# Row spreads, sample-state outer products and sample-state products of a hybrid decoder step: fp32r and column tiles

## The chip, the cores and the metric

One core of one Trainium2 chip runs the whole program. The metric is the device time of one execution in microseconds. The kernel before took 1665.42 us (median of three runs, 1665.4 to 1666.57).

## What is computed

The reference is one decoder layer for 256 prompt tokens and 8 sample tokens (d_model 1024, 8 heads): a gated-delta branch (GDN) and a latent-attention branch (MLA) on one normalised input, merged by gates, then an MLP. All data is fp32. The change touches the recurrence of the samples, the row scalings of the GDN branch and one row scaling of the MLA branch:

```python
def gdn_recurrent(q, k, v, g, beta, s0):      # the samples: 8 tokens, 8 heads, one step
    s = jnp.exp(g_t)[..., None, None] * s
    u = b_t[..., None] * (v_t - jnp.einsum('bhk,bhkv->bhv', k_t, s))
    s = s + jnp.einsum('bhk,bhv->bhkv', k_t, u)
    return s, jnp.einsum('bhk,bhkv->bhv', q_t, s)

def l2_normalize(x):                          # q and k of GDN, per token and head
    return x * lax.rsqrt(jnp.sum(jnp.square(x), axis=-1, keepdims=True) + EPS)
```

Activations lie channel by token (128 partitions of channels, 264 columns of tokens: 256 prompt, 8 sample). A factor per token is therefore a row, and a row has to be spread over 128 partitions before VectorE can multiply by it.

## The kernel before

**Stages.** A front stage (to about 140 us) computes the down projections. Then 128 cache pages are worked off (to about 1314 us), and the last stage runs the gate, output and MLP matrices. TensorE's operands of the large products are split into a high and a low fp32r part, and three fp32r products stand for one of fp32.

**The page loop.** Each page n has two halves, and `keys(n, half)` issues 12 fp32r products of 512 columns for each (lines 1729 to 1731). In front of each half, `beside(i)` with i = 2n + half issues a piece of other work, on TensorE, VectorE and ScalarE alike. Every engine runs its own instruction list in order, and semaphores tie them. `beside` holds first the prompt attention (`front_pe`, i under 29), then from i = 35 four head pairs b = 0 to 3 of 52 slots k each (`pair_pe`, `pair_dve`, `pair_act`).

**Two side banks.** Products of `beside` go in turn to two PSUM banks in the order of the list SIDE_A. `begin_a(name)` waits until the bank's last user but one was read, `a_bank(name)` on VectorE waits for the product. Small transposes go through one more bank (SIDE_B).

**The places that the change touches**, by slot k of a pair:
- `spread_row` (line 1791): one fp32 product whose stationary operand is one column of the identity, broadcast to 128 columns; out comes a row on all partitions. Slots 18, 19 (`gr`, 64 rows of `rw`), 21, 22 (`br`, 64 rows), 23, 24 (`lb`, two each, 4 rows of `lr`), 51 (`ob`, two, 2 rows of `lr`): 10 in a pair. The same form stands at line 1941 for `nope` (16 rows of `nrow`, 256 columns, two in each of the slots i = 10 to 17).
- `newton` (lines 1209 to 1218): VectorE turns the square root of a row into its reciprocal with one Newton step; the `lb` spreads wait for the one of slot 22, the `ob` spreads for the one of slot 50.
- `kqs` (line 1890, slot 28): for each of 8 samples and 2 heads, the 128 x 128 sample state is the stationary operand and the two columns q and k are the moving one: 16 fp32 products of two columns.
- `krow`, `urow` (slots 30, 32): transposes of 16 columns; ScalarE copies the rows to `urow`.
- `state_out` (line 1808, slots 40, 42, 45, 47): k outer u for four state blocks at once, one fp32 product with 16 rows of contraction and 512 columns. `masked_rows` (line 1324) zeroes the rows of u that belong to other blocks.

An fp32 product stands in the trace as two records (it streams its columns twice), an fp32r product as one.

Of the kernel before, what the change touches and what calls it, by code (L numbers as in the profile page):

```python
# [21 lines left out]
P = 128  # L22
D = 1024
TP = 256
# [45 lines left out]
C_LVT = _col(P)  # L70
C_ALL = _at


def constants():

    c = np.zeros((P, C_ALL), np.float32)
    k, m = np.arange(P)[:, None], np.arange(P)[None, :]
    c[:, C_ID] = k == m
    c[:, C_BD] = k // 64 == m // 64
    c[:, C_ROT] = np.where((k == m + 32) & (m % 64 < 32), -1.0, 0) + ((k == m - 32) & (m % 64 >= 32))  # L80
    c[:, C_ONE] = 1.0
    inv = np.power(np.float32(10000.0), -np.arange(0, ROPE, 2, dtype=np.float32) / np.float32(ROPE)).astype(np.float32)
    pos = np.concatenate([np.arange(TP), np.full(NS, PAST)]).astype(np.float32)
# [12 lines left out]
    c[0:8, C_RSC] = SCALE  # L96
    c[8:16, C_RSC] = 1
    c[0:2, C_RSQ] = 128 ** -0.5
    c[2:4, C_RSQ] = 1
    c[:, C_LVT] = c[:, C_LVL[0]].T  # L100
    return c
# [14 lines left out]
PAIR_A = ([f"p{j}" for j in range(6)] + ["gr0", "gr1", "l2r", "br0", "br1", "lb0", "lb1", "lb2", "lb3", "qk", "kk", "qks", "x0", "x1", "kqs", "t1", "u1"])  # L116
# [39 lines left out]
def build(nc, I, O):  # L156
    C_in, ctx = I["consts"], ExitStack()
    with ctx:
# [35 lines left out]
        qeff, e = place("qeff", [P, NS, 5, 16], F32, taken["rsq"][0])  # L194
        assert e <= taken["rsq"][1]
# [49 lines left out]
        ltok = [place("ltok0", [P, LW], F32, taken["ukT01"][0])[0], place("ltok1", [P, LW], F32, taken["ukT67"][0])[0], place("ltok2", [P, LW], F32, taken["sq"][0])[0]]  # L245
        nrow, e2 = place("nrow", [16, T], F32, taken["sq"][0] + 4 * T * 4)
# [16 lines left out]
        assert e <= C_NEG.stop * 4  # L263
        lr, e = place("lr", [8, 2, T], F32, taken["krT"][0])
# [30 lines left out]
        bwl, o = place("bwl", [P, KC, P], F32R, o)  # L295
        rw, o = place("rw", [64, T], F32, o)
# [11 lines left out]
        sm, o = place("sm", [P, 8, 2 * NS], F32, o)  # L308
        lt3, o = place("lt3", [8, T], F32, o)
# [16 lines left out]
        umask, e = place("umask", [16, 4, P], F32, e)  # L326
        urow, e = place("urow", [16, 2, P], F32, e)
# [276 lines left out]
        def _(act):  # L604
# [159 lines left out]
            def pair_act(b, k):  # L764
# [37 lines left out]
                if k == 30:  # L802
                    nc.scalar.activation(urow[:, 0, :], rows_out(f"krow_{b}")[0:16, 0:P], ACT.Copy).then_inc(S("b_read"), 1)
                if k == 32:
                    nc.scalar.activation(urow[:, 1, :], rows_out(f"urow_{b}")[0:16, 0:P], ACT.Copy).then_inc(S("b_read"), 1)
# [110 lines left out]
        def _(v):  # L916
# [180 lines left out]
            def front_dve(i):  # L1097
# [42 lines left out]
                if i == 9:  # L1140
                    V.tensor_copy(snew[:], a_bank("snew")[:, 0:64]).then_inc(S("a_read"), 1)
# [20 lines left out]
            def decay_steps(i):  # L1162
# [17 lines left out]
                if i == 4:  # L1180
                    pair_low(0)
                if i == 5:
                    V.tensor_copy(bg[:].rearrange("p n c -> p (n c)"), a_bank("bg")[:, 0:128]).then_inc(S("a_read"), 1)

# [49 lines left out]
            def pair_dve(b, k):  # L1234
# [46 lines left out]
                if k == 25:  # L1281
                    V.tensor_tensor(dt_[:], four(bank("qk")), dt_[:], ALU.mult).then_inc(S("a_read"), 1)
                    V.tensor_tensor(lT[:], four(bank("kk")), lT[:], ALU.mult).then_inc(S("a_read"), 1)
                    v.wait_ge(S("a_read"), a_count(f"lb3_{b}"))
                    V.tensor_copy(small(1), sample_of(2)).then_inc(S("sample_ready"), 1)
                    V.tensor_tensor(small(2), sample_of(0), sample_of(2), ALU.mult).then_inc(S("sample_ready"), 1)
                if k == 26:
# [7 lines left out]
                    link(V.scalar_tensor_tensor(col2[:, 0:2], colb[:, 0, 1, :], -1.0, bg[:, 1, 2 * b:2 * b + 2], ALU.mult, ALU.mult))  # L1295
                if k == 27:
# [6 lines left out]
                if 28 <= k < 40 and k % 2 == 1:  # L1303
# [3 lines left out]
                    V.tensor_tensor(U_[:], U_[:], four(bank(f"u{s_}")), ALU.subtract).then_inc(S("a_read"), 1)  # L1307
                if k == 28:
                    kq = bank("kqs")[:, 0:4 * NS].rearrange("p (s h t) -> p s h t", s=NS, t=2)
                    egs = eg[:, :, TP:T].rearrange("p h s -> p s h")  # L1310
                    V.tensor_tensor(small(3), kq[:, :, :, 1], egs, ALU.mult)
                    V.tensor_tensor(small(4), kq[:, :, :, 0], egs, ALU.mult).then_inc(S("a_read"), 1)
                    v.wait_ge(S("a_read"), a_count(f"kqs_{b}"))
                    link(V.tensor_tensor(small(3), sample_of(4), small(3), ALU.subtract))
                    V.tensor_tensor(small(5), small(3), small(7), ALU.mult).then_inc(S("sample_ready"), 1)
# [5 lines left out]
                def masked_rows(m):  # L1321
                    v.wait_ge(S("b_read"), b_count(f"urow_{b}"))
                    v.wait_ge(S("conv_out"), 32 * b + 32)
                    V.tensor_tensor(umask[:], urow[:, 1, :].unsqueeze(1).to_broadcast([16, 4, P]),
                                    consts[0:16, C_ID.start + 4 * m:C_ID.start + 4 * m + 4].unsqueeze(2).to_broadcast([16, 4, P]), ALU.mult).then_inc(S("umask_ready"), 1)
# [267 lines left out]
        def _(pe):  # L1593
# [196 lines left out]
            def spread_row(name, rows_, col, moving):  # L1790
                a_done(mm(begin_a(name)[:, 0:T], consts[0:rows_, C_ID.start + col:C_ID.start + col + 1].to_broadcast([rows_, P]), moving, start=True, stop=True))  # L1791

            def pair_pe(b, k):
# [38 lines left out]
                if k in (18, 19):  # L1832
                    pe.wait_ge(S("g_ready"), 1)
                    pe.wait_ge(S("beta_ready"), 1)
                    spread_row(f"gr{k - 18}_{b}", 64, 32 + 2 * b + k - 18, rw[:])
# [6 lines left out]
                if k in (21, 22):  # L1842
                    spread_row(f"br{k - 21}_{b}", 64, 2 * b + k - 21, rw[:])
# [6 lines left out]
                if k in (23, 24):  # L1850
                    pe.wait_ge(S("row_rstd"), 2 * b + 1)
                    for c in range(2 * (k - 23), 2 * (k - 23) + 2):
                        spread_row(f"lb{c}_{b}", 4, c, lr[0:4, 0])
# [4 lines left out]
                if k == 26:  # L1858
# [24 lines left out]
                if k == 28:  # L1883
                    pe.wait_ge(S("sst_landed"), 16 * NS * (b + 1))
                    qks = qkv[:, 0:4, :].rearrange("p (t h) n -> p h n t", t=2)
                    p_ = begin_a(f"kqs_{b}")
                    for s_ in range(NS):
                        for hh in range(2):
                            at_ = 2 * (2 * s_ + hh)
                            i = mm(p_[:, at_:at_ + 2], sst[:, s_, hh, :], qks[:, hh, TP + s_, :], start=True, stop=True)  # L1890
                    a_done(i)
                if k == 30:
                    b_done(nc.tensor.transpose(begin_b(f"krow_{b}")[0:16, 0:P], sm[:, 1], ident))
                if k == 32:
                    pe.wait_ge(S("sample_ready"), 4 * b + 3)
                    b_done(nc.tensor.transpose(begin_b(f"urow_{b}")[0:16, 0:P], sm[:, 5], ident))
# [37 lines left out]
                if k == 51:  # L1934
                    pe.wait_ge(S("row_rstd"), 2 * b + 2)
                    for hh in range(2):
                        spread_row(f"ob{hh}_{b}", 2, hh, lr[0:2, 0])

            def front_pe(i):
# [47 lines left out]
                if F_NOPE <= i < F_NOPE + H:  # L1987
                    for n_ in (0, H):
                        h = n_ + i - F_NOPE
                        a_done(spread(begin_a(f"nope{h}")[:, 0:TP], nrow[:, 0:TP], 16, h))  # L1990
# [214 lines left out]
```

## Time and profile before

| | |
|---|---|
| time, median of three | 1665.42 us |
| time of the profiled execution | 1668.4 us |
| its span, first to last instruction | 1666.6 us |
| PE busy | 1628.4 us |
| DVE, ACT, POOL busy | 886.2, 649.5, 201.6 us |
| mean granted TensorE clock | 0.990 |

The profiled execution is 1.8 us longer than its span and 3.0 us longer than the median. PE is TensorE's matmuls, DVE VectorE, ACT ScalarE, POOL GpSimd. Durations of matmul records overlap, since they include filling and draining; what a matmul costs is read from one start to the next start.

### The profile page before, as it was taken

To read this page: it belongs to the slowest core of one execution; us is meant where nothing else is said; L and a number is where in the kernel's file an instruction comes from. 1 tells how busy PE (TensorE), PEld (TensorE's weight loads), DVE (VectorE), ACT (ScalarE), POOL (GpSimd) and SP (SyncE) were. 2 spreads that over 40 slices of the span, in tenths; PEclk is the share of its full clock that TensorE was granted. 3 is DMA by queue.
4 is the path that set the end of the run, shared out by engine and by line. 5 is a ranking of instruction groups with operands and counts; after the bars stand their busy time and mean duration, and the time that the engine had idled before them with its cause. 6 is when DMAs were issued, how large, how long until landed. Compare 5 with 4: busy or idle time off the path is not lost.

```text
span 1666.6 us, 26110 instructions
## 1 busy us (share of the span) xinstructions
PE 1628.4 (98%) x10140; PEld 1331.9 (80%) x10140; DVE 886.2 (53%) x1636; ACT 649.5 (39%) x981; POOL 201.6 (12%) x104
## 2 busy tenths in 40 slices
PE   6899999999999999999999999999999999999998
PEld 5777777886877777877877877877877899999998
DVE  5855444455445555354555445545444565777643
ACT  2233356345324445223454234353334344344431
POOL 0000202111111211111111112111112200000000
PEclk9999999999999999999999999999999999999999
DMA  7421102421012321102320013211013346545551
GB/s 248 138 75 34 31 20 56 126 68 29 29 29 59 107 81 30 29 29 59 92 68 29 29 30 96 83 30 29 29 32 105 127 166 214 177 155 187 185 181 52
DMA packets 111621, 140.79 MB, mean 84 GB/s; under 512 B 13648, under 2 KB 60272, under 8 KB 111368
## 3 DMA queue, kind: packets, MB, share of 16 engines
q1 hardware_dynamic: 106902, 137.13, 26.3%
q10 hardware_dynamic: 4602, 2.05, 0.5%
q8 instruction: 79, 1.29, 0.3%
q14 instruction: 38, 0.31, 0.1%
HBM read 132.61 MB, written 6.74 MB: 84 GB/s over the span
## 4 chain that ended last, share of the span: by engine, by line
PE 93%; DVE 4%; ACT 1%; ACTq 1%; issue 0%; DVEq 0%
PE ps L1729 15%; PE ps L1731 14%; PE ps L1730 14%; PE ps L2125 5%; PE ps L2126 5%; PE ps L2127 5%; PE ps L1720 4%; PE ps L1765 2%; PE ps L1749 2%; PE ps L2071 1%; PE ps L1816 1%; PE ps L2072 1%; PE ps L1815 1%; PE ps L2073 1%; PE ps L1817 1%; PE ps L1791 1%
## 5 line engine op out<-in xcount | busy, mean ns | idle before, releaser
L1729 PE MATMUL ps<-ukh,cTh 128*128 128x512 f32 x1024 | 426.8, 417 | 0.1
L1048 DVE TENSOR_REDUCE kss<-ksq 128x4 f32<-128x512 f32 x256 | 175.5, 685 | 463.3 <-ACT ksq L690 462.9
L1731 PE MATMUL ps<-ukh,cTl 128*128 128x512 f32 x1024 | 404.7, 395 | 0.0
L1730 PE MATMUL ps<-ukl,cTh 128*128 128x512 f32 x1024 | 403.7, 394 | 0.0
L690 ACT ACTIVATE ksq<-ps 128x512 f32<-128x512 f32 x256 | 152.8, 597 | 564.9 <-PE ps L1731 564.8
L595 POOL TENSOR_TENSOR rk<-kss,mhalf 128x32 f32<-128x32 f32 x32 | 178.3, 5570 | 548.0 <-DVE kss L1423 548.0
L1729 PEld LDWEIGHTS ps<-ukh,cTh 128*128 128x128 f32 x1024 | 194.6, 190 | 61.4 <-issue 27.2
L1731 PEld LDWEIGHTS ps<-ukh,cTl 128*128 128x128 f32 x1024 | 194.3, 190 | 45.0
L1730 PEld LDWEIGHTS ps<-ukl,cTh 128*128 128x128 f32 x1024 | 195.3, 191 | 33.5
L1426 DVE TENSOR_TENSOR wl<-wraw,wh 128x2048 fp32r<-128x2048 f32 x44 | 100.8, 2291 | 76.3 <-ACT wh L877 76.1
L877 ACT ACTIVATE wh<-wraw 128x2048 fp32r<-128x2048 f32 x44 | 84.3, 1916 | 133.8 <-PE ps L2127 126.0
L1044 DVE TENSOR_TENSOR cTl<-cTr,cTh 128x512 fp32r<-128x512 f32 x128 | 87.9, 687 | 14.4 <-ACT cTh L684 13.8
L2125 PE MATMUL ps<-Ah,wh 128*128 128x264 f32 x320 | 91.1, 285 | 1.2 <-DVE wl L1426 1.2
L1720 PEld LDWEIGHTS ps<-consts_sb,craw 128*128 128x128 f32 x512 | 59.1, 141 | 41.4 <-issue 33.1
L2127 PE MATMUL ps<-Ah,wl 128*128 128x264 f32 x320 | 90.8, 284 | 0.0
L2126 PE MATMUL ps<-Al,wh 128*128 128x264 f32 x320 | 90.7, 283 | 0.0
L684 ACT ACTIVATE cTh<-cTr 128x512 fp32r<-128x512 f32 x128 | 80.8, 631 | 4.1
L1720 PE MATMUL ps<-consts_sb,craw 128*128 128x128 f32 x512 | 80.4, 279 | 0.8 <-ACT cTr L681 0.8
L681 ACT ACTIVATE cTr<-ps 128x512 f32<-128x512 f32 x128 | 76.1, 595 | 0.5 <-PE ps L1720 0.3
L2127 PE MATMUL ps<-Hh,wl 128*128 128x264 f32 x256 | 72.9, 285 | 0.0
L2125 PE MATMUL ps<-Hh,wh 128*128 128x264 f32 x256 | 72.8, 284 | 0.0
L2126 PE MATMUL ps<-Hl,wh 128*128 128x264 f32 x256 | 72.8, 284 | 0.0
(445 smaller groups left out, 2865.1 us busy)
## 6 DMA issues: line engine op xcount, KB each, us to landing
craw<-cache_mla SPq DMA_DIRECT2D x128, 288.0 KB, 3.1
wraw<-w_in SPq DMA_DIRECT2D x16, 1024.0 KB, 4.9
wraw<-w_up SPq DMA_DIRECT2D x16, 1024.0 KB, 5.4
wraw<-w_down SPq DMA_DIRECT2D x16, 1024.0 KB, 4.9
braw<-w_in SPq DMA_DIRECT2D x24, 512.0 KB, 3.8
sst<-state_gdn SPq DMA_DIRECT2D x32, 128.0 KB, 3.6
gdn_sample<-sst SPq DMA_DIRECT2D x32, 128.0 KB, 2.1
wraw<-w_ya SPq DMA_DIRECT2D x4, 1024.0 KB, 5.0
```

Source lines behind the costliest of these rows:

```text
L595: nc.gpsimd.tensor_tensor(rk[:, y], kss[:, y], mhalf[:], ALU.pow).then_inc(S("rk_ready"), 1)
L690: nc.scalar.activation(ksq[:, half_], ps[:, k % 3, :], ACT.Square).then_inc(S("ksq_ready"), 1)
L1044: V.tensor_tensor(cTl[:, n % 2], cTr[:, :, tokens(n)], cTh[:, n % 2].bitcast(F32), ALU.subtract).then_inc(S("ct_lo"), 1)
L1048: V.tensor_reduce(kss[:, n // 4 % 2, n % 4, 4 * half_:4 * half_ + 4], ksq[:, half_].rearrange("p (h d) -> p h d", h=4), AX, ALU.add).then_ ...
L1426: V.tensor_tensor(wl2[:, ns % 2], wraw2[:, (ns - NM) % 4], wh2[:, ns % 2].bitcast(F32), ALU.subtract).then_inc(S("w_lo"), 1)
L1720: k = nc.tensor.transpose(trp[:, c, :], craw[:, n % RING, P * c:P * c + P], ident)
L1729: mm(out, cTh[:, n % 2, c], ukh[:, c, cols], start=c == 0, stop=False)
L1730: mm(out, cTh[:, n % 2, c], ukl[:, c, cols], start=False, stop=False)
L1731: i = mm(out, cTl[:, n % 2, c], ukh[:, c, cols], start=False, stop=c == 3)
L2125: mm(out, w_hi, mh[:, kc, :], start=first and kc == 0, stop=False)
L2126: mm(out, w_hi, ml[:, kc, :], start=False, stop=False)
L2127: k = mm(out, w_lo, mh[:, kc, :], start=False, stop=last and kc == 3)
```

## The change

Five edits, in one diff:
1. `spread_row` issues two fp32r products into one accumulation, a high and a low part of the row; its stationary column comes from `idr`, a rounded copy of the identity. VectorE makes the parts with `split` (a copy and a subtraction): for `rw` once, for `nrow` once (slot i = 9), and for `lr` at the end of each `newton`, whose consumers now wait for the split. `nope` uses `spread_row` too.
2. `kqs` moves from slot 28 to slot 26. The q and k columns of the samples are gathered in `sm` (32 columns) and are the stationary operand, 8 columns at a time; the state is the moving operand, 4 fp32 products of 512 columns, each to its own 32 partitions of the bank.
3. VectorE copies that bank to `X_` (slot 26), TensorE transposes it (4 blocks, `kqsT`, slot 27), and VectorE picks the wanted entries (slot 27, as before in slot 28).
4. `krow` and `urow` transpose three copies of the 16 columns (96 columns, from `ksrc`, `usrc`). ScalarE writes them rounded to fp32r (`kst`, `ust`) and one third raw (`kraw`), and VectorE turns one third into the low part (slots 31, 33).
5. `state_out` becomes one fp32r product with 96 rows: k high with u high, k low with u high, k high with u low, stacked. `umask` is 96 rows of fp32r.

```diff
             def newton(rows_, count, scale, sem):
...
-                V.scalar_tensor_tensor(x, y, scale, t_, ALU.mult, ALU.mult).then_inc(S(sem), 1)
+                link(V.scalar_tensor_tensor(x, y, scale, t_, ALU.mult, ALU.mult))
+                split(x, lrh[0:rows_], lrl[0:rows_], sem)
...
                 if k == 26:
+                    V.tensor_copy(X_[:].rearrange("p u n -> p (u n)"), bank("kqs")).then_inc(S("a_read"), 1)
+                if k == 31:
+                    v.wait_ge(S("b_read"), b_count(f"krow_{b}"))
+                    V.tensor_tensor(kst[32:64], kraw[32:64], kst[32:64].bitcast(F32), ALU.subtract).then_inc(S("kst_ready"), 1)
...
-            def spread_row(name, rows_, col, moving):
-                a_done(mm(begin_a(name)[:, 0:T], consts[0:rows_, C_ID.start + col:C_ID.start + col + 1].to_broadcast([rows_, P]), moving, start=True, stop=True))
+            def spread_row(name, rows_, col, high, low, width=T):
+                out, one = begin_a(name)[:, 0:width], idr[0:rows_, col:col + 1].to_broadcast([rows_, P])
+                mm(out, one, high, start=True, stop=False)
+                a_done(mm(out, one, low, start=False, stop=True))
...
                 def state_out(m):
+                    pe.wait_ge(S("kst_ready"), b + 1)
                     pe.wait_ge(S("umask_ready"), 4 * b + m + 1)
-                    a_done(mm(begin_a(f"out{m}_{b}"), urow[:, 0, :], umask[:].rearrange("p h n -> p (h n)"), start=True, stop=True))
+                    a_done(mm(begin_a(f"out{m}_{b}"), kst[:], umask[:].rearrange("p h n -> p (h n)"), start=True, stop=True))
...
                     a_done(mm(begin_a(f"qks_{b}")[:, 0:2 * NS], ones, sm[:, 2], start=True, stop=True))
+                    pe.wait_ge(S("sst_landed"), 16 * NS * (b + 1))
+                    p_ = begin_a(f"kqs_{b}")
+                    for j in range(4):
+                        i = mm(p_[32 * j:32 * j + 8, :], sm[:, 0:2].rearrange("p a n -> p (a n)")[:, 8 * j:8 * j + 8],
+                               sst[:, 2 * j:2 * j + 2].rearrange("p s h v -> p (s h v)"), start=True, stop=True)
+                    a_done(i)
                 if k == 27:
                     read("kk")
                     four("x0", 4, lambda out, w: nc.tensor.transpose(out, lT[:, w, :], ident))
+                    read("kqs")
+                    four("kqsT", 4, lambda out, w: nc.tensor.transpose(out, X_[:, w, :], ident))
...
-                if k == 28:
-                    pe.wait_ge(S("sst_landed"), 16 * NS * (b + 1))
-                    qks = qkv[:, 0:4, :].rearrange("p (t h) n -> p h n t", t=2)
-                    p_ = begin_a(f"kqs_{b}")
-                    for s_ in range(NS):
-                        for hh in range(2):
-                            at_ = 2 * (2 * s_ + hh)
-                            i = mm(p_[:, at_:at_ + 2], sst[:, s_, hh, :], qks[:, hh, TP + s_, :], start=True, stop=True)
-                    a_done(i)
                 if k == 30:
-                    b_done(nc.tensor.transpose(begin_b(f"krow_{b}")[0:16, 0:P], sm[:, 1], ident))
+                    b_done(nc.tensor.transpose(begin_b(f"krow_{b}")[0:96, 0:P], ksrc[:].rearrange("p r c -> p (r c)"), ident))
```

## Rows read from the trace of the kernel before

**Rows 1.** The page's busy times: us, share of the span, instructions.

```profile
PE 1628.4 (98%) x10140; PEld 1331.9 (80%) x10140; DVE 886.2 (53%) x1636; ACT 649.5 (39%) x981; POOL 201.6 (12%) x104
```

**Rows 2.** Groups of instructions: form, xrecords | busy us, mean ns | idle.

```profile
L1808 PE MATMUL ps<-umask,urow 16*128 16x512 f32 x32 | 17.9, 640 | 0.0
L1941 PE MATMUL ps<-nrow,consts_sb 16*128 16x256 f32 x32 | 9.0, 400 | 0.0
```

**Rows 3.** Chain that ended last, pair 0 slot 24: start us, us, line, xrecords.

```profile
402.89 0.23 PE ps L1731
403.12 1.08 PE ps L1791 x4
404.20 0.43 PE ps L1729
```

**Rows 4.** The same chain, pair 0 slot 19: a single spread.

```profile
379.67 0.64 PE ps L1791 x2
380.31 0.43 PE ps L1729
```

**Rows 5.** The same chain, pair 0 slot 40: an outer product.

```profile
485.33 1.05 PE ps L1808 x2
486.38 0.43 PE ps L1729
```

**Rows 6.** The same chain: one fp32r product of 264 columns.

```profile
784.28 0.12 PE ps L1816
```

**Rows 7.** The same chain, pair 2 slot 28: the sample-state products.

```profile
912.96 3.47 PE ps L1890 x32
916.43 0.34 PE ps L1729
```

**Rows 8.** The same chain, pair 3: 512 fp32r columns at the lower clock.

```profile
1159.72 0.43 PE ps L1729
```

**Rows 9.** Stretches: us, busy us of PE, PEld, DVE, ACT, POOL; clock, DMA.

```profile
425.35:432.18 6.83, 6.83 (x21) 4.78 (x25) 0.61 (x4) 0.52 (x1) 0.00 (x0) 0.50 0.00 0
...
780.33:783.75 3.42, 3.42 (x9) 2.63 (x8) 0.42 (x1) 0.00 (x0) 0.00 (x0) 0.50 0.07 24
...
1159.21:1162.63 3.42, 3.42 (x11) 2.64 (x10) 0.00 (x0) 0.31 (x1) 0.45 (x1) 0.50 0.00 0
...
1265.00:1268.40 3.40, 2.65 (x11) 1.97 (x12) 2.80 (x6) 0.79 (x2) 0.00 (x0) 1.00 0.85 251
```

**Rows 10.** The chain again: a run of transposes, then products on four column tiles.

```profile
383.30 0.44 PE ps L1757 x4
...
388.55 1.00 PE ps L1765 x8
389.55 0.48 PE ps L1720 x3
```

**Rows 11.** Timeline, VectorE, end of the Newton step in pair 1 slot 50.

```profile
777.67 0.28 DVE L1217 TENSOR_SCALAR lt<-lt 2x264 f32<-2x264 f32 x1
778.00 0.42 DVE L1218 SCALAR_TENSOR_TENSOR lr<-lr,lt 2x264 f32<-2x264 f32 x1
```

**Rows 12.** Waits of TensorE: us in total, times, longest.

```profile
PE ps L1791 <- DVE lr L1218: 3.3, 4, 1.3
```

**Rows 13.** Timeline, both engines, pair 0 slots 50 and 51.

```profile
532.80 0.42 DVE L1218 SCALAR_TENSOR_TENSOR lr<-lr,lt 2x264 f32<-2x264 f32 x1
...
533.38 0.48 PE L1791 MATMUL ps<-lr,consts_sb 2*128 2x264 f32 x1
```

**Rows 14.** Timeline, both engines, pair 1 slots 22 and 23.

```profile
641.03 0.48 DVE L1218 SCALAR_TENSOR_TENSOR lr<-lr,consts_sb,lt 4x264 f32<-4x264 f32 x1
...
642.57 0.48 PE L1791 MATMUL ps<-lr,consts_sb 4*128 4x264 f32 x1
```

**Rows 15.** Timeline, both engines, pair 1 slots 26 and 27.

```profile
660.61 0.15 DVE L1295 SCALAR_TENSOR_TENSOR col<-colb,bg 128x2 f32<-128x2 f32 x1
...
661.44 0.38 PE L1867 MATMUL ps<-consts_sb,lT 128*128 128x128 f32 x2
```

More of the change, by code:

```diff
@@ L70 @@
 C_LVT = _col(P)
+C_THIRDS = _col(16)
 C_ALL = _at
@@ L100, in constants @@
     c[:, C_LVT] = c[:, C_LVL[0]].T
+    c[0:96, C_THIRDS] = k[0:96] % 32 == m[:, 0:16]
     return c
@@ L115 @@
 B_START, B_SLOTS = F_END + 6, 52
-PAIR_A = ([f"p{j}" for j in range(6)] + ["gr0", "gr1", "l2r", "br0", "br1", "lb0", "lb1", "lb2", "lb3", "qk", "kk", "qks", "x0", "x1", "kqs", "t1", "u1"])
+PAIR_A = ([f"p{j}" for j in range(6)] + ["gr0", "gr1", "l2r", "br0", "br1", "lb0", "lb1", "lb2", "lb3", "qk", "kk", "qks", "kqs", "x0", "kqsT", "x1", "t1", "u1"])
 for _s in range(2, LEVELS):
@@ L194, in build @@
         qeff, e = place("qeff", [P, NS, 5, 16], F32, taken["rsq"][0])
+        idr, e = place("idr", [64, 64], F32R, e)
         assert e <= taken["rsq"][1]
@@ L245, in build @@
         ltok = [place("ltok0", [P, LW], F32, taken["ukT01"][0])[0], place("ltok1", [P, LW], F32, taken["ukT67"][0])[0], place("ltok2", [P, LW], F32, taken["sq"][0])[0]]
+        nrowh, e2 = place("nrowh", [16, TP], F32R, taken["ltok0"][1])
+        assert e2 <= taken["ukT01"][1]
+        nrowl, e2 = place("nrowl", [16, TP], F32R, taken["ltok1"][1])
+        assert e2 <= taken["ukT67"][1]
         nrow, e2 = place("nrow", [16, T], F32, taken["sq"][0] + 4 * T * 4)
@@ L263, in build @@
         assert e <= C_NEG.stop * 4
+        rwh, e = place("rwh", [64, T], F32R, C_NEG.start * 4)
+        assert e <= C_NEG.stop * 4
+        lrl, e = place("lrl", [8, T], F32R, taken["krT"][0] + 4 * T)
         lr, e = place("lr", [8, 2, T], F32, taken["krT"][0])
@@ L295, in build @@
         bwl, o = place("bwl", [P, KC, P], F32R, o)
+        rwl, _ = place("rwl", [64, T], F32R, o)
         rw, o = place("rw", [64, T], F32, o)
@@ L308, in build @@
         sm, o = place("sm", [P, 8, 2 * NS], F32, o)
+        lrh, _ = place("lrh", [8, T], F32R, o)
         lt3, o = place("lt3", [8, T], F32, o)
@@ L325, in build @@
         uu, e = place("uu", [P, 2, CH], F32, e)
-        umask, e = place("umask", [16, 4, P], F32, e)
-        urow, e = place("urow", [16, 2, P], F32, e)
+        umask, e = place("umask", [96, 4, P], F32R, e)
+        kst, e = place("kst", [96, P], F32R, e)
+        ust, e = place("ust", [96, P], F32R, e)
+        kraw, e = place("kraw", [96, P], F32, max(e, taken["tail"][1]))
+        ksrc, e = place("ksrc", [P, 3, 32], F32, e)
+        usrc, e = place("usrc", [P, 3, 32], F32, e)
         assert e <= TOP, e
@@ L1140, in front_dve @@
                 if i == 9:
+                    V.tensor_copy(idr[:], consts[0:64, C_ID.start:C_ID.start + 64])
+                    split(nrow[:, 0:TP], nrowh[:], nrowl[:], "nope_split")
                     V.tensor_copy(snew[:], a_bank("snew")[:, 0:64]).then_inc(S("a_read"), 1)
@@ L1181, in decay_steps @@
                     pair_low(0)
+                    V.memset(ksrc[:], 0.0)
+                    V.memset(usrc[:], 0.0).then_inc(S("src_clear"), 1)
                 if i == 5:
                     V.tensor_copy(bg[:].rearrange("p n c -> p (n c)"), a_bank("bg")[:, 0:128]).then_inc(S("a_read"), 1)
+                    v.wait_ge(S("beta_ready"), 1)
+                    split(rw[:], rwh[:], rwl[:], "rw_split")
             def conv(b, j):
@@ L1284, in pair_dve @@
                     v.wait_ge(S("a_read"), a_count(f"lb3_{b}"))
-                    V.tensor_copy(small(1), sample_of(2)).then_inc(S("sample_ready"), 1)
+                    for j in range(2):
+                        V.tensor_copy(sm[:, 0:2].rearrange("p a (s h t) -> p (a s) h t", h=2, t=2)[:, :, :, j], sample_of(2 * j))
+                    if b == 0:
+                        v.wait_ge(S("src_clear"), 1)
+                    V.tensor_copy(ksrc[:, :, 0:16].rearrange("p r (s h) -> p r s h", h=2), sample_of(2).unsqueeze(1).to_broadcast([P, 3, NS, 2])).then_inc(S("sample_ready"), 1)
                     V.tensor_tensor(small(2), sample_of(0), sample_of(2), ALU.mult).then_inc(S("sample_ready"), 1)
@@ L1307, in pair_dve @@
                     V.tensor_tensor(U_[:], U_[:], four(bank(f"u{s_}")), ALU.subtract).then_inc(S("a_read"), 1)
-                if k == 28:
[L1309 to L1313, printed above, removed]
+                if k == 27:
+                    bank("kqsT")
+                    at_ = B_PAIR + SIDE_A.index(f"kqsT_{b}") % 2
+                    kq = ps[:, at_:at_ + 2, :].rearrange("p b n -> p (b n)")[:, 0:520].rearrange("p (i x) -> p i x", x=130)[:, :, 0:128]
+                    kq = kq.rearrange("p (a h) (j r) -> p a h j r", h=2, r=32)
+                    egs = eg[:, :, TP:T].rearrange("p h (j a) -> p a h j", a=2)
+                    V.tensor_tensor(sm[:, 3].rearrange("p (j a h) -> p a h j", a=2, h=2), kq[:, :, :, :, 1], egs, ALU.mult)
+                    V.tensor_tensor(sm[:, 4].rearrange("p (j a h) -> p a h j", a=2, h=2), kq[:, :, :, :, 0], egs, ALU.mult).then_inc(S("a_read"), 1)
+                if k == 28:
+                    v.wait_ge(S("a_read"), a_count(f"kqsT_{b}"))
                     link(V.tensor_tensor(small(3), sample_of(4), small(3), ALU.subtract))
-                    V.tensor_tensor(small(5), small(3), small(7), ALU.mult).then_inc(S("sample_ready"), 1)
+                    link(V.tensor_tensor(small(5), small(3), small(7), ALU.mult))
+                    V.tensor_copy(usrc[:, :, 0:16], sm[:, 5].unsqueeze(1).to_broadcast([P, 3, 2 * NS])).then_inc(S("sample_ready"), 1)
                 if k == 30:
@@ L1321, in masked_rows @@
                 def masked_rows(m):
-                    v.wait_ge(S("b_read"), b_count(f"urow_{b}"))
+                    v.wait_ge(S("ust_ready"), b + 1)
                     v.wait_ge(S("conv_out"), 32 * b + 32)
-                    V.tensor_tensor(umask[:], urow[:, 1, :].unsqueeze(1).to_broadcast([16, 4, P]),
-                                    consts[0:16, C_ID.start + 4 * m:C_ID.start + 4 * m + 4].unsqueeze(2).to_broadcast([16, 4, P]), ALU.mult).then_inc(S("umask_ready"), 1)
+                    V.tensor_tensor(umask[:], ust[:].bitcast(F32).unsqueeze(1).to_broadcast([96, 4, P]),
+                                    consts[0:96, C_THIRDS.start + 4 * m:C_THIRDS.start + 4 * m + 4].unsqueeze(2).to_broadcast([96, 4, P]), ALU.mult).then_inc(S("umask_ready"), 1)
                 def state_out(m):
@@ L1832, in pair_pe @@
                 if k in (18, 19):
[L1833 to L1835 removed]
+                    pe.wait_ge(S("rw_split"), 1)
+                    spread_row(f"gr{k - 18}_{b}", 64, 32 + 2 * b + k - 18, rwh[:], rwl[:])
                 if k == 20:
@@ L1987, in front_pe @@
                 if F_NOPE <= i < F_NOPE + H:
+                    pe.wait_ge(S("nope_split"), 1)
                     for n_ in (0, H):
                         h = n_ + i - F_NOPE
-                        a_done(spread(begin_a(f"nope{h}")[:, 0:TP], nrow[:, 0:TP], 16, h))
+                        spread_row(f"nope{h}", 16, h, nrowh[:], nrowl[:], TP)
                 if F_NOPE <= i < F_NOPE + 6:
```

20 lines of the change are left out of this document (14 added, 6 removed).

## The prediction, made before the changed kernel ran

> **What bounds the kernel now.** First the page's busy times [rows 1]: TensorE is busy in 98% of the span, VectorE in 53%, ScalarE in 39%. So a change pays what it takes off TensorE's own line, and it costs whatever makes TensorE wait. Next the groups of instructions [rows 2] for what the touched products are: all fp32, two records for each product. Their busy and mean times overlap with neighbours, so they are no price. The price is read from the chain that ended last, which in the page loop is TensorE almost without a break: each piece there is the time that it adds. Then the waits of TensorE [rows 12]: in the page loop it waits for only one thing, the Newton step that the `lb` and `ob` spreads need, 3.3 us in four waits. Last the stretches with their granted clock [rows 9]: 0.50, the lower level of 1.2 GHz, in stretches that begin right behind the sample-state products of `kqs`, and in one behind an `ob` spread.
>
> **What a block costs.** A product of the keys with 512 columns takes 0.23 us in the chain, one directly behind a spread or an outer product 0.43 [rows 3, 5]. So a block costs its own piece and 0.20. Two spreads: 1.08 + 0.20 = 1.28 for four records [rows 3]. One spread: 0.64 + 0.20 = 0.84 for two [rows 4]. The difference, 0.44 for two records, makes 0.22 a record, and 0.84 - 0.44 = 0.40 stays for each block whatever it streams: its edges. An outer product costs 1.05 + 0.20 = 1.25 [rows 5]. Its two records of 512 columns are 2 x 0.22 x 512/264 = 0.85, which again leaves 0.40.
>
> **Edit 1, the spreads.** An fp32r product of 264 columns costs 0.12 [rows 6]. A spread goes from two records of 0.22 to two of 0.12: it saves 0.20, and the edges stay, since the rows of contraction stay 64, 16, 4 and 2. The 40 spreads of the pairs (10 in each of four) save 8.0. The 16 of `nope` [rows 2] have 256 columns and save 0.19 each, 3.0. Sum 11.0 us. The row for 0.12 has 128 rows of contraction; none of the trace has fp32r with fewer. I take 0.12, and the other end is under the rivals.
>
> **Edit 5, the outer products.** 16 of them (32 records, [rows 2]) go from 1.25 to one fp32r product of 512 columns, 0.23 [rows 3]. Whether the edges of 0.40 stay with 96 rows no row shows: blocks of 2 to 64 rows have them, the keys with 128 rows don't. Without edges the saving is 1.02 each, 16.3 in all; with them 0.62 each, 9.9. I take 16.3, because 96 rows can't share the array with a second product, while up to 64 could, and keep 9.9 for the range. On this the Trainium skill has a rule (TensorEngine Tiling (Array Packing), Key Properties and Available Configurations): a change of tiling mode drains the engine, and there is row tiling for 64 and for 32 rows only. By it the edges go with 96 rows, which is the 16.3; by the nearest row alone, 16 rows, it would be the 9.9. The same rule speaks against edit 2, which brings a new tiling mode into slot 26; the price of that is in its row below.
>
> **Edit 2 and 3, the sample-state products.** Before: 3.47 us [rows 7], and 0.34 in place of 0.23 for the next, 3.58. After: four fp32 products on four column tiles. The same shape costs 1.00 for its eight records, and the three transposes behind it 0.48 in place of 0.33 (four in 0.44) [rows 10], so 1.15 to 1.20; I take 1.18. The transposes of `X_` are four more, 0.44 [rows 10]. So 3.58 - 1.62 = 1.96 a pair, 7.8 in all. If the four tiles didn't overlap they would cost 3.4 and the edit would save nothing. The `krow` and `urow` transposes keep their length of 128 streamed columns: between nothing and 0.1 either way, taken as nothing.
>
> **What the clock gives back.** Behind each of the four `kqs` runs, in which TensorE streams two columns per weight load for 3.5 us and more, the granted clock is 0.50: from 425.35 for 6.83 us, the same in pair 1 from 667.69, and 3.42 in pairs 2 and 3 [rows 9]. In it a key product takes 0.43 and not 0.23 [rows 8]. The four stretches sum to 20.5 us, and half of that, 10.2 us, is lost. Behind the shape that replaces it [rows 10], which already runs twice in each group of four pages, the chain shows key products at 0.23 again. I take all 10.2.
>
> **What VectorE adds.** The split behind each Newton step is a copy and a subtraction with 4 or 2 rows: by the last two steps, 0.33 from the start of L1217 to that of L1218 and 0.42 and a little for the operation itself [rows 11], so 0.78 until TensorE is released (0.7 to 0.9). Behind the waiting TensorE instruction everything is queued, the 12 key products first. Where TensorE waits already (`lb` of pairs 0 and 2, `ob` of pairs 1 and 3, [rows 12]) it counts in full: 4 x 0.78 = 3.1. At `lb` of pairs 0 and 2 TensorE also comes 0.2 earlier, because the `br` spread ahead is shorter while the Newton step's start hangs on the key norms before it: +0.4. At `ob` of pairs 0 and 2 the step ends at 533.22 and the spread starts at 533.38 [rows 13]: of 0.78 some 0.62 is left, +1.2. At `lb` of pairs 1 and 3 it ends at 641.51 and the spread starts at 642.57 [rows 14]: 1.06 covers 0.78 + 0.2. Sum +4.8 us.
>
> The copy of `X_` comes behind L1295, which ends at 660.76, and takes about 0.7 like VectorE's other steps of 512 columns; TensorE reaches the transposes of `X_` after the new products and `x0`, at 661.44 + 1.18 + 0.44 = 663.1 [rows 15]. That is 1.6 us of cover: nothing. If the cover were gone, each us would cost 4 over the pairs. The remaining small steps (gathering q and k, `ksrc`, `usrc`, the two subtractions, ScalarE's two extra copies, the splits of `rw` and `nrow`) lie a slot or more ahead of their readers, behind 12 key products of 0.23, 2.8 us: nothing, at most 1 us in all.
>
> **A new fall of the clock.** In pair 1 TensorE stood 1.3 us in front of the `ob` spreads, and from 780.33 the clock was 0.50 for 3.42 us. In pair 3 it stood as long, and the stretch from 1265.00 shows 1.00 [rows 9, 12]. With 2.1 us of standing both may fall. I take one fall more, +1.7 us (half of 3.42); the bounds are -1.7 and, if all six waits bring one, +8.5.
>
> **The sum.** -11.0 - 16.3 - 7.8 - 10.2 + 4.8 + 1.7 = -38.8 us. On the profiled execution, 1668.4 us with its span of 1666.6, that is 1629.6. The median of the runs shown lies 3.0 lower, 1665.42, so 1626.6.
>
> **The rivals.**
> - *The edges stay at 96 rows*: 6.4 us less gain, 1633.0. For it: every block with fewer than 128 rows in the trace has them. Against it: see edit 5.
> - *The clock falls anyway behind `kqs`*: its 8 columns of output per tile are few, and it now stands next to the transposes of `kt` and `qks`. Then the 10.2 us aren't won: 1636.8. Against it: the clock is 1.00 behind the same shape elsewhere.
> - *More falls at the waits*: TensorE stands up to 2.1 us at six places instead of 1.3 at most. Five falls more in place of one, 8.5 and not 1.7: 1633.4.
> - *Slower: the fp32r products with few rows stream their columns twice like fp32.* Then the change doesn't do what it says. A spread becomes four records of 0.22 instead of two, +0.44 for 56 spreads = +24.6; the outer products save only edges or nothing (0). With -7.8 - 10.2 + 4.8 + 1.7 that is +13.1: 1678.5. It decides from about 0.32 per fp32r record of 264 columns on: 56 x (0.64 - 0.44) are the 11.5 that the other terms leave. For it: no row with fp32r and few rows. Against it: all fp32r products in the trace are one record, and fp32 with few rows streams at the pace of fp32 with many.
> - *The gains of TensorE are used up by another engine's lateness*: VectorE at 53% and ScalarE at 39% speak against more than a few us; it lies within the range.
>
> **How the numbers follow.** Forecast 0.58; edges stay 0.14; clock falls behind `kqs` 0.12; more falls at the waits 0.09; slower by the doubled streaming 0.03; gains given back for a reason that I don't see, ending near 1665, 0.04. The range goes down to 1618: no fall at the `ob` spreads (3.4), waits 1.5 shorter, and some 3.7 for prices that are read to 0.01 or 0.02 us and used on some 200 records. It goes up to 1640: the edges stay or the clock isn't won, with two or more of the further falls. A measurement of this kernel tells about 0.2%, 3.3 us, from no change. Faster 0.95, same 0.02, slower 0.03.
>
> **What would show it.** In the changed profile: one record per outer product and 0.23 in the chain, and 0.23 for the key product behind it (0.43 if the edges stay); `lb` blocks of 0.68 in place of 1.08; eight records of `kqs` in about 1.0 us and no stretch of 0.50 behind them; TensorE's waits for the split at six places, about 8 us together and up to 2.1 each; about two stretches of 0.50 in the page loop, behind the `ob` spreads. The prediction is wrong if fp32r records with few rows take over 0.2 us each, if TensorE waits at the transposes of `X_`, or if the clock falls at places where it didn't.

## The result

The changed kernel takes 1628.21 us (median of four runs, 1627.37 to 1629.12) against 1665.94 for the kernel before (median of four; the 1665.42 further up are that of the first three); the ratio is 0.9776, 95% interval 0.9764 to 0.9789. That is 37.7 us less, where 38.8 were forecast, and inside the range of 1618 to 1640. The profiled execution took 1627.37 us with a span of 1625.6, 41.0 less than the span before.

The page's busy times of the changed kernel, as [rows 1]:

```profile
PE 1581.3 (97%) x10044; PEld 1306.9 (80%) x10044; DVE 898.1 (55%) x1683; ACT 651.3 (40%) x989; POOL 202.2 (12%) x104
```

TensorE has shed 47 us of busy time, and the span only 41: the rest is standing, 4.9 us more of it in the page loop and about 1 us in the front stage. TensorE's waits for the split, as [rows 12], and the end of the Newton step in the chain of pair 0, as [rows 11]:

```profile
PE ps L1836 <- DVE lrl L977: 8.2, 6, 2.0
```
```profile
394.65 0.49 DVE lr L1244
...
395.16 0.30 DVE lrh L976
...
395.48 0.43 DVE lrl L977
```

Six waits instead of four, 8.2 us instead of 3.3. From the end of L1244 (395.14) to the end of L977 (395.91) are 0.77 us: the split.

The chain at TensorE's blocks (start us, us, line, records). In this kernel L1836 and L1837 are the high and the low product of a spread, L1773 to L1775 the key products, L1914 `kqs`, L1921 its transposes and L1855 the outer product. A single spread of slot 18, two spreads of slot 23 behind a wait with what follows them, and the two of slot 24, which don't wait, as [rows 3, 4]:

```profile
370.99 0.32 PE ps L1836
371.31 0.12 PE ps L1837
```
```profile
395.96 0.38 PE ps L1836
396.34 0.12 PE ps L1837
...
396.71 0.43 PE ps L1773
...
397.60 0.43 PE ps L1773
398.03 0.43 PE ps L1774
...
401.24 0.31 PE ps L1836
401.55 0.12 PE ps L1837
401.67 0.12 PE ps L1836
401.80 0.12 PE ps L1837
401.92 0.44 PE ps L1773
```

A spread is 0.44 where it was 0.64 (0.32 + 0.12). Two are 0.68 where they were 1.08 (401.24 to 401.92), and 0.75 behind a wait. The key product behind them is still 0.43 or 0.44 instead of 0.23: the edges stayed. The two lines from 397.60 are another 0.43, that of the lower clock, which began at 397.47. The sample-state products of slot 26, their transposes in slot 27 and two outer products, as [rows 5, 7]:

```profile
410.85 0.97 PE ps L1914 x8
411.82 0.43 PE ps L1773
...
417.15 0.44 PE ps L1921 x4
417.59 0.23 PE ps L1773
```
```profile
477.92 0.24 PE ps L1855
478.16 0.23 PE ps L1773
...
485.90 0.26 PE ps L1855
486.16 0.24 PE ps L1773
```

`kqs` costs 0.97 + 0.20 and 0.44 for the transposes; an outer product 0.24 to 0.26 with nothing behind it. The stretches at the lower level of 1.2 GHz in the page loop, and between them a stretch behind the wait of 2.04 us in pair 1, which shows 1.00 (columns as [rows 9]):

```profile
397.47:400.89 3.42, 3.42 (x10) 2.60 (x8) 1.03 (x3) 0.00 (x0) 0.00 (x0) 0.50 0.00 0
...
757.00:760.50 3.50, 3.50 (x17) 2.86 (x18) 1.89 (x4) 0.00 (x0) 0.00 (x0) 1.00 0.35 105
1226.91:1230.30 3.39, 3.39 (x10) 2.61 (x9) 0.45 (x1) 0.00 (x0) 0.00 (x0) 0.50 0.58 171
```

Two stretches, 6.8 us, where the kernel before had five, 23.9 us. None lies behind `kqs`. Both lie behind a wait: of 1.40 us at `lb` of pair 0 and of 2.04 at `ob` of pair 3. Behind the wait of 2.04 in pair 1 the clock stayed at 1.00.

### The profile page after: what moved, and what is told of

The parts are those of the page before. It is cut to its first block, busy times and chain, and to the rows that moved or that the text cites. A ratio compares the mean times of both kernels' runs of the same rounds, so it can differ in the third digit from the quotient of the medians.

```text
span 1625.6 us, 25985 instructions
## 1 busy us (share of the span) xinstructions
PE 1581.3 (97%) x10044; PEld 1306.9 (80%) x10044; DVE 898.1 (55%) x1683; ACT 651.3 (40%) x989; POOL 202.2 (12%) x104
## 4 chain that ended last, share of the span: by engine, by line
PE 91%; DVE 5%; ACT 2%; ACTq 1%; issue 1%; DVEq 0%
PE ps L1773 15%; PE ps L1775 14%; PE ps L1774 14%; PE ps L2171 5%; PE ps L2172 5%; PE ps L2173 5%; PE ps L1764 4%; PE ps L1809 2%; PE ps L1793 2%; PE ps L2117 1%; PE ps L2119 1%; PE ps L1862 1%; PE ps L2118 1%; PE ps L1863 1%; PE ps L1864 1%; PE ps L1936 1%
## 5 line engine op out<-in xcount | busy, mean ns | idle before, releaser
L1773 PE MATMUL ps<-ukh,cTh 128*128 128x512 f32 x1024 | 421.6, 412 | 0.1
L1775 PE MATMUL ps<-ukh,cTl 128*128 128x512 f32 x1024 | 403.0, 394 | 0.0
L1773 PEld LDWEIGHTS ps<-ukh,cTh 128*128 128x128 f32 x1024 | 193.3, 189 | 46.4 <-issue 9.5
L1775 PEld LDWEIGHTS ps<-ukh,cTl 128*128 128x128 f32 x1024 | 193.1, 189 | 43.5
L700 ACT ACTIVATE cTh<-cTr 128x512 fp32r<-128x512 f32 x128 | 80.9, 632 | 4.1
```

The costliest lines, as they stand in the source:

```text
L1773: mm(out, cTh[:, n % 2, c], ukh[:, c, cols], start=c == 0, stop=False)
L1775: i = mm(out, cTl[:, n % 2, c], ukh[:, c, cols], start=False, stop=c == 3)
```

## The experiments

The theory: TensorE's line sets the time, and four things add up on it: the pieces in the chain, the edges of blocks with few rows, the standing in front of the Newton step, and half of each stretch at the lower clock. Ten kernels took one or two of them away or put them back; an eleventh run is the changed kernel itself. All are edits of the changed kernel, so its line numbers are a few lower or higher in them. They were measured in three series, each on another chip. The kernel before ran in all three (medians 1665.9, 1665.5 and 1666.0 us), so what the chip makes is some 0.5 us. The changed kernel ran again in the first series only, and its 1627.68 us is the yardstick for all. Where a difference of medians needs taking apart, the profiles are compared by the page loop's length, from the start of the first key product of line L1773 to that of the last: 1143.7 us in the changed kernel, both times, and 1183.2 in the kernel before. A stretch of 0.50 lasts 3.4 us unless another length is given and costs half of it, 1.7 us.

### The waits and the spreads

**The changed kernel again.** No edit.

> The changed kernel, unedited, beside the other three. Both theories: 1628.2 us (1627 to 1629.5), TensorE waiting six times and 8.2 us in all for the split behind the Newton step. It also shows how the stretches at the lower granted clock move from one execution to the next: in the first profile of it they began at 124.4, 397.5 and 1226.9 us.

Measured: 1627.68 us (1626.36 to 1628.92), ratio 0.9765 (0.9752 to 0.9779). Six waits, 8.1 us. The stretches of 0.50 began at 80.9, 398.4 and 1227.8: the two behind waits at the same waits, the one in the front stage elsewhere.

**No split behind the Newton step.** `spread_whole` is the fp32 form that the kernel before has.

```diff
-                link(V.scalar_tensor_tensor(x, y, scale, t_, ALU.mult, ALU.mult))
-                split(x, lrh[0:rows_], lrl[0:rows_], sem)
+                V.scalar_tensor_tensor(x, y, scale, t_, ALU.mult, ALU.mult).then_inc(S(sem), 1)
...
-                        spread_row(f"lb{c}_{b}", 4, c, lrh[0:4], lrl[0:4])
+                        spread_whole(f"lb{c}_{b}", 4, c, lr[0:4, 0])
```

> The changed kernel, but the lb and ob spreads are one fp32 product again and the Newton step has no split behind it. Theory (pieces on TensorE's line and waits both count in full): 24 spreads cost 0.20 more each, +4.8; the six waits fall from 8.2 to about 3.3 us, -4.9; the two falls of the clock behind these waits may go, 0 to -3.4. So 1624.8 to 1628.2. Rival (the wait of TensorE is made up for later, since VectorE and ScalarE catch up in it): the shorter waits bring nothing and the time is 1633.

Measured: 1628.72 us (1625.82 to 1628.89), 0.5 above the expected band and far from the rival's 1633. The wait row:

```profile
PE ps L1834 <- DVE lr L1244: 3.8, 4, 1.3
```

It is 3.8, not 3.3: the `br` spreads ahead are shorter than in the kernel before (with those in fp32 too, two runs further down, it is 3.4). So the fp32r form of the 24 spreads behind a Newton step wins 4.8 us of pieces and loses 4.3 of standing. It is worth nothing, within what can be measured.

**Only the spreads that wait are whole.**

```diff
+                i = V.scalar_tensor_tensor(x, y, scale, t_, ALU.mult, ALU.mult)
+                i.then_inc(S(sem), 1)
+                if rows_ == 4:
+                    v.wait_ge(S(sem), count)
+                    split(x, lrh[0:rows_], lrl[0:rows_], "lr_split")
...
+                        if k == 23:
+                            spread_whole(f"lb{c}_{b}", 4, c, lr[0:4, 0])
```

> The changed kernel, but the spreads for which TensorE stands waiting (lb of slot 23, ob of slot 51) are one fp32 product and don't wait for the split; the lb of slot 24, by which time the split is long done, stay two fp32r products. Theory: 16 spreads cost 0.20 more each, +3.2; waits -4.9; falls of the clock 0 to -3.4. So 1623.1 to 1626.5, faster than the changed kernel by 1.7 to 5. Rival (waits are made up for later): 1631.4, slower than the changed kernel.

Measured: 1625.57 us (1623.14 to 1627.04), ratio 0.9754 (0.9740 to 0.9767): inside the band, the waits 3.8 us again. The intervals of this kernel and the changed one overlap, so it is the waits' row that carries the verdict, and not the 2.1 us.

**All spreads in fp32.** As above for all 56, with no use of the split parts.

```diff
-                    spread_row(f"gr{k - 18}_{b}", 64, 32 + 2 * b + k - 18, rwh[:], rwl[:])
+                    spread_whole(f"gr{k - 18}_{b}", 64, 32 + 2 * b + k - 18, rw[:])
```

> The changed kernel with edit 1 undone: all 56 spreads are one fp32 product, no splits. Theory: +11.0 for the pieces, -4.9 for the waits, 0 to -3.4 for the clock: 1630.9 to 1634.3. Rival 1 (waits are made up for later): 1639.2. Rival 2 (the fp32r spreads bring nothing, because the blocks are bound by their edges): 1620 to 1623. The difference of e4 and e2 is the 32 spreads that nobody waits for, 6.3 us by the theory.

Measured: 1632.26 us (1630.5 to 1636.25), inside the theory's band, away from both rivals. Edit 1 as a whole is worth 4.6 us of the 37.7. The profile shows where the rest of its 11.0 us went: the waits are 3.4 us in place of 8.1, and no stretch of 0.50 lies in the page loop in place of two.

### The edges

**Outer products in fp32 with 16 rows.**

```diff
-                    a_done(mm(begin_a(f"out{m}_{b}"), kst[:], umask[:].rearrange("p h n -> p (h n)"), start=True, stop=True))
+                    a_done(mm(begin_a(f"out{m}_{b}"), kst[0:16].bitcast(F32), umask[0:16].bitcast(F32).rearrange("p h n -> p (h n)"), start=True, stop=True))
```

> The changed kernel, but the state outer products are one fp32 product with 16 rows of contraction again (the first third of the stacked rows; the two low parts are left out of the result). VectorE's and ScalarE's work stays. Theory: each costs 1.25 again and not 0.23, +16.3: 1644 to 1645. Rival (the edges had stayed with 96 rows): the difference would be only 9.9, 1638.

Measured: 1646.6 us (1645.29 to 1647.96). 18.9 above the changed kernel of the other series, where 16.3 were expected. The chain has the 1.25 of before:

```profile
479.22 1.05 PE ps L1855 x2
480.27 0.43 PE ps L1773
```

This profile has three stretches of 0.50 in the page loop and one behind it (1385.3), and the changed kernel two and none: two more, worth 3.4 us. The granted clock is 0.994 in all four executions and 0.996 in all of the changed kernel, so this covers the 2.6 us that are over.

**Outer products with 64 of the 96 rows.**

```diff
+                    a_done(mm(begin_a(f"out{m}_{b}"), kst[0:64], umask[0:64].rearrange("p h n -> p (h n)"), start=True, stop=True))
```

> The changed kernel, but the state outer products take 64 of the 96 stacked rows, still fp32r and 512 columns (k high with u low is left out of the result). Less is computed. Theory (blocks of up to 64 rows have edges of 0.40, since the engine is emptied when it goes over to such a block and back; 96 rows have none): each costs 0.63 instead of 0.23, +6.4 for 16, 1634 to 1635. Rival (only the columns streamed count, whatever the rows; the edges of before came from fp32): no change, 1628.

Measured: 1635.77 us (1633.9 to 1638.88). A third of the rows less, the same columns, and 8.1 us more. The chain:

```profile
479.81 0.43 PE ps L1855
480.24 0.43 PE ps L1773
```

0.43 + 0.20 = 0.63 where 96 rows have 0.24 and nothing: the 0.40 of edges, and neither fp32 nor the number of records has a part in it. The page loop is 4.5 us longer than the changed kernel's (1148.2), with one stretch of 0.50 in it instead of two: 6.2 for the blocks, where 16 x 0.40 are 6.4. What is left of the 8.1 us lies outside the loop: a longer wait in the front stage and a stretch of 0.50 at 1372.7. By the Trainium skill (TensorEngine Tiling (Array Packing), Key Properties) a change of tiling mode drains the engine, and its list of configurations (Available Configurations) has row tiling for 64 and for 32 rows only. The trace agrees as far as it goes: 64 rows pay 0.40, 96 rows nothing. That it is a drain, no run shows.

**Spreads with 128 rows.** The tiles get rows of zeros, once, and the one-hot stationary operand has 128 rows.

```diff
-                out, one = begin_a(name)[:, 0:width], idr[0:rows_, col:col + 1].to_broadcast([rows_, P])
+                out, one = begin_a(name)[:, 0:width], idr[:, col:col + 1].to_broadcast([P, P])
...
+                    V.memset(rwh[64:128].bitcast(F32), 0.0)
+                    V.memset(rwl[64:128].bitcast(F32), 0.0)
+                    V.memset(lrh[:].bitcast(F32), 0.0)
+                    link(V.memset(lrl[:].bitcast(F32), 0.0))
```

> The changed kernel, but each of the 56 spreads contracts over 128 rows: the same two fp32r products, with rows of zeros below the 64, 16, 4 or 2 rows of data. Nothing is left out, and TensorE multiplies more zeros. Theory (the 0.40 of edges comes from going over to fewer rows and back): the 36 blocks lose their edges, 36 x 0.40 = 14.4 less, with the six waits as before: 1613 to 1615. A block of two spreads is 0.48 in the chain, the key product behind it 0.23. Rival (the edges belong to the first product behind another dtype, operand or semaphore): no change, 1628.

Measured: 1617.3 us (1616.1 to 1618.99), ratio 0.9708 (0.9693 to 0.9724): 10.4 below the changed kernel, and 2 to 4 above the band. Where TensorE doesn't wait, the edges are gone as expected; where it does, the first product takes 0.39 as in the changed kernel:

```profile
372.44 0.12 PE ps L1842
372.57 0.12 PE ps L1843
372.69 0.23 PE ps L1779
...
391.39 0.39 PE ps L1842
391.77 0.12 PE ps L1843
391.89 0.12 PE ps L1842
392.02 0.12 PE ps L1843
392.14 0.23 PE ps L1779
```

So behind a wait only the 0.20 at the block's end is won. And there are eight such waits now, since TensorE comes earlier:

```profile
PE ps L1842 <- DVE lrl L977: 9.3, 8, 2.0
```

Three of the `nope` blocks win only their front too, because the product behind them (L2051) has 64 rows itself and keeps its edge:

```profile
173.97 0.12 PE ps L1843
174.09 0.20 PE ps L2051
174.29 0.43 PE ps L1779
```

25 x 0.40 + 11 x 0.20 - 1.2 = 11.0 is what this makes, against 10.4 measured. The profile also has one stretch of 0.50 in the page loop instead of two, so there it should be 12.7, and the loop is 11.3 shorter (1132.4). About 1.4 us of the edges are not accounted for.

### The clock

**The state stationary, two columns moving**, in slot 28 (edits 2 and 3 undone). VectorE's copy and the transposes of `X_` are gone with them.

```diff
+                    for s_ in range(NS):
+                        for hh in range(2):
+                            at_ = 2 * (2 * s_ + hh)
+                            i = mm(p_[:, at_:at_ + 2], sst[:, s_, hh, :], qks[:, hh, TP + s_, :], start=True, stop=True)
```

> The changed kernel with edits 2 and 3 undone: kqs in slot 28, the state stationary, two columns moving, 32 records, no copy and no transposes. Theory: +7.8 for the pieces and +10.2 for the clock, which falls to 0.50 behind each of the four runs again, 20 us of it in all: 1646, and 1642 to 1646 if some stretches are shorter. Rival (the falls weren't caused by these products): +7.8, 1636, with the clock at 1.00 behind them.

Measured: 1643.67 us (1642.17 to 1646.42), 16.0 above the changed kernel. The run in pair 0 and the four stretches behind the runs:

```profile
420.14 3.47 PE ps L1930 x32
423.61 0.34 PE ps L1767
```
```profile
424.80:428.20 3.40, 3.40 (x12) 2.01 (x14) 0.00 (x0) 0.35 (x1) 0.00 (x0) 0.50 0.00 0
660.30:663.70 3.40, 3.40 (x10) 2.62 (x9) 0.21 (x2) 0.00 (x0) 0.45 (x1) 0.50 0.00 0
902.70:906.10 3.40, 3.40 (x9) 2.61 (x9) 0.51 (x3) 0.00 (x0) 0.00 (x0) 0.50 0.03 5
1138.20:1141.60 3.40, 3.40 (x11) 2.72 (x11) 0.80 (x5) 0.00 (x0) 0.00 (x0) 0.50 0.00 0
```

Four stretches again, but 3.4 us each and not 6.8 in two of them: 6.8 us of time here where the kernel before lost 10.2. This profile has four more in the page loop, behind waits, where the changed kernel has two. By these the loop should be 7.8 + 6.8 + 3.4 = 18.0 us longer; it is 17.6 (1161.3). The profiled execution is the slowest of the four (1646.42 us, granted clock 0.989); the others show 0.991 and 0.992, so fewer stretches, and 16.0 as the median.

**The same with 128 columns moving.** The operand is another part of q, so the sample outputs are not the reference's.

```diff
+                            at_ = 128 * (s_ % 4)
+                            i = mm(p_[:, at_:at_ + 128], sst[:, s_, hh, :], qkv[:, hh, 0:128], start=True, stop=True)
```

> As e7, but each of the 16 products streams 128 columns of q instead of two columns (another result, so the sample outputs aren't the reference's). The records stay 32, and each takes about 0.11 us either way, by the load of its stationary operand or by its columns. Theory (the clock falls because TensorE streams next to nothing for 3.5 us): the run takes 3.5 to 3.6 us as in e7, the clock stays 1.00 behind it, time 1636, some 10 below e7. Rival (the clock falls because of the stretch itself, its waits or its loads of the stationary operand): as e7, 1646.

Measured: 1634.47 us (1632.95 to 1636.82): 64 times the columns, and 9.2 us less. The run, and the stretches behind the runs of pairs 0 and 3:

```profile
417.14 3.57 PE ps L1930 x32
420.71 0.23 PE ps L1767
```
```profile
420.70:427.50 6.80, 6.80 (x45) 5.04 (x44) 2.96 (x10) 2.38 (x4) 2.36 (x1) 1.00 0.15 44
...
1129.20:1136.00 6.80, 6.80 (x42) 5.94 (x41) 3.46 (x9) 1.72 (x3) 0.45 (x1) 1.00 0.00 0
```

3.57 against 3.47 us, the same records, the same loads of the stationary operand, the same waits for the split (8.1 us), and the clock stays at 1.00 behind all four. What made it fall in the kernel before was that TensorE streamed two columns for each load in these runs. The page loop is 1151.7 us, 8.0 more than the changed kernel's, with two stretches of 0.50 in either: this is the price of the pieces alone, forecast at 7.8. Of the 9.2 us between this kernel and the last one the four stretches are 6.8; behind waits the last one's profile has four stretches and this one's two. Each record takes 0.11 either way. By the Trainium skill (TensorE: Matmul & The Clock Gate, LDWEIGHTS (loading the stationary operand)) a load takes its columns over 1.2 GHz, which for 128 makes an estimate of 0.107 us, and the 3.47 us of 32 records, 0.108 each, agree. At the lower clock they don't: the run in pair 1 of the kernel before, 2.7 us of it at 0.50, took 4.68 us, about 0.20 for each record there.

### The waits taken away

**The Newton step a slot earlier.**

```diff
-                if k == 21:
+                if k == 20:
                     act.wait_ge(S("a_read"), a_count(f"l2r_{b}"))
...
-                if k == 22:
+                if k == 21:
                     newton(4, 2 * b + 1, consts[0:4, C_RSQ], "row_rstd")
```

and the same for `ob`, from slots 49 and 50 to 48 and 49.

> The changed kernel, but the square root and the Newton step with its split come one slot earlier on ScalarE and VectorE (slots 20 and 21 for lb, 48 and 49 for ob). Nothing is left out. Theory (the six waits of 8.2 us count in full, and the falls of the clock behind them come from them): no wait for the split, no fall in the page loop, -8.2 and 0 to -3.4: 1616 to 1620. Rival (the earlier step only moves the lateness: VectorE's 4.2 us come into slots 21 and 49, and TensorE waits there for the br spread's bank or for the key norms): 1626 to 1628 with waits for another instruction of VectorE or ScalarE.

Measured: 1618.04 us (1617.05 to 1619.47), ratio 0.9712 (0.9698 to 0.9726), 9.6 below the changed kernel. No stretch of 0.50 and no wait for the split lies in the page loop. The last wait of TensorE before the loop's end is this, in front of the first key product:

```profile
PE ps L1764 <- ACT cTr L697: 0.8, 1, 0.8
```

The page loop is 11.7 us shorter (1132.0), and 8.1 for the waits and 3.4 for the two stretches make 11.5: both count in full. The median shows 9.6, since this profile has a stretch of 0.50 behind the loop (1353.5) that the changed kernel doesn't have. The Newton step's 4.3 us on VectorE were taken up by its slack in slot 21: 55% busy is enough room, it only lay in the wrong slot.

**Both**, the earlier step and the 128 rows.

> e9 and e10 together, nothing left out. Theory: -8.2 for the waits, 0 to -3.4 for the clock, -14.4 for the edges: 1602 to 1606, if the two don't meet; TensorE comes some 0.4 to 0.8 us earlier to the lb spreads because of the shorter gr and br blocks, so one or two short waits may come back, +1. Rival (VectorE's order becomes the bound): 1608 to 1614.

Measured: 1603.1 us (1601.64 to 1604.27), ratio 0.9620 (0.9605 to 0.9634), inside the band. No wait on the Newton step, no fall of the clock in the page loop, and no edges of the spreads' own. The loop is 24.4 us shorter (1119.3), where 8.1 + 3.4 + 33 x 0.40 + 3 x 0.20 are 25.3. It is 25 us faster than the changed kernel and 63 faster than the kernel before.

## Why the prediction was right, and where it was off

- **Spreads, -11.0.** Right in size: 0.64 to 0.44 and 1.08 to 0.68 in the chain, to the hundredth, and the fp32r products with 64, 16, 4 and 2 rows take the 0.12 that only a row with 128 rows had shown. The rival of doubled streaming is dead. (Its threshold of 0.32 per record makes 11.2 us and not the 11.5 that the other terms leave; this decides nothing.)
- **Outer products, -16.3 or -9.9.** The open end was the edges with 96 rows. They are gone: 0.24 and 0.23 behind. The 64-row kernel shows that this is the number of rows and not the type. The 16-row kernel gives 18.9 with two more stretches of the lower clock in it.
- **Sample-state products, -7.8.** 0.97 + 0.20 + 0.44 = 1.61 a pair against 1.62, and the kernel with 128 columns puts the whole at 8.0. The copy of `X_` was covered, as forecast.
- **Clock, -10.2.** None behind `kqs`. Its cause, products that stream two columns, was argued from what stood ahead of the stretches; the kernel with 128 columns shows it. Where the prediction has the stretches begin right behind the runs, the trace of before has them from 2.7 us before a run's end (pair 1, at 667.69) to 1.2 us behind it (pair 3):

```profile
422.44 3.86 PE ps L1890 x32
...
665.68 4.68 PE ps L1890 x32
```

  In pairs 0 and 1 the runs themselves were stretched by it, beyond the 3.47 us of pair 2. The sum doesn't suffer, since half of each stretch was counted whatever lay in it. Put back, the products cost 6.8 us of clock and not 10.2, since two of the stretches came back half as long. How long TensorE stays at the lower level behind such a run isn't a constant of the run; the 10.2 were one execution's.
- **Waits, +4.8.** 8.2 - 3.3 = 4.9, at the six places named, with 0.77 for the split. That they count in full is shown by the earlier Newton step: 11.7 us of the page loop for 8.1 of waits and 3.4 of clock.
- **One more fall, +1.7.** Two were forecast, behind the `ob` waits of pairs 1 and 3; two came, but at `lb` of pair 0 and `ob` of pair 3. The sum was right and the place half wrong, and by the prediction's own sign (the clock falls where it didn't) the fall at `lb` is a miss. That the number came out is in part luck. The length of the wait alone doesn't tell: 1.40 us had one and 2.04 had none. Other kernels have the same six waits within 0.01 us and other falls: only at `lb` of pair 0 with 64 rows in the outer products, only at `ob` of pairs 1 and 3 with 128 columns in `kqs`. What decides between two such waits stays open.
- **The sum.** The page loop's share of the clock is (23.9 - 6.8)/2 = 8.5, as forecast. The page loop fell by 39.5 us against the sum of 38.8, and the profiled span by 41.0. What is over is mainly 1.7 outside the page loop, where the kernel before had two stretches of 0.50 (63.5 and 1405.0 us) and this one has one (124.4); no part of the change runs on TensorE there. The medians differ by 37.7 only, since the profiled execution of the kernel before was 2.5 us above its median of 1665.94 and that of the changed kernel 0.8 below its own.

What the prediction missed was the use of its own numbers: it counted 0.40 us of edges on 36 blocks and a wait of up to 2 us in front of six, and took both as given. Together they were 25 us, two thirds of the gain of the change.

## What to carry to other kernels

Price a small product by its block in the chain, and look at what stays when its streaming is taken away: here the edges of blocks with up to 64 rows cost as much as three fp32r products of 264 columns (0.40 us against 0.12), and rows of zeros up to 128 remove them, unless a product with few rows stands next to them. A run of products that stream two columns each over a stationary operand of 128 cost twice here, once by its loads (3.47 us) and once by the clock (1.7 to 3.4 us); exchange the operands. And a faster form that needs one more step on another engine belongs where nobody waits for that step: move the step a slot earlier first.

## What the runs showed of the hardware that few would expect

- More rows of contraction made a block faster: 96 rows 0.24, 64 rows 0.63 with its edges; and the same two products over 128 rows 0.24 instead of 0.64.
- More columns made the kernel faster: 128 columns in place of two, 3.57 us instead of 3.47 for the run, and 9.2 us less in the whole.
- The first fp32r product of 264 columns behind a wait takes 0.38 us with 2 or 4 rows and 0.39 with 128 rows, against 0.12 for 128 rows in the stream.
- The stretches at the lower clock behind waits change place between kernels whose waits are the same: at `lb` of pair 0 and `ob` of pair 3 in the changed kernel, at `ob` of pairs 1 and 3 in the one with 128 columns, at `lb` of pair 0 alone in the one with 64 rows.
